# Where a two-network kernel splits three weight tiles, and 24 TensorE products that nobody reads

## The reference, cut to what matters

```
first network, layer l:
  mod = silu(c) @ w_ada[l] + b_ada[l]                  # shifts, scales, gates
  h = rms_norm(x) * (1 + scale_m) + shift_m
  x = x + gate_m * hybrid_mixer(h)                     # w_in, attention, gated linear attention, w_out
  h = rms_norm(x) * (1 + scale_f) + shift_f
  x = x + gate_f * moe(h)      # each token: one of 4 groups, 2 of its 8 experts
                               # an expert: (silu(h @ w_gate) * (h @ w_up) * weight) @ w_down
second network, layer l:
  x = x + mixer(rms_norm(x))                           # four kinds of attention, w_in_2, w_out_2
  x = x + relu(rms_norm(x) @ w_up_2)**2 @ w_down_2
```

## Time and profile before

| | |
|---|---|
| three timed runs | 1749.98, 1756.49, 1759.61 us; median 1756.49 |
| the profiled execution | 1746.62 us, of it a span of 1744.8 us |
| mean granted TensorE clock | 0.976 |
| busy over the span | PE 93%, DVE 67%, ACT 53%, POOL 6% |
| the two expert loops | some 300 us each (about 250 to 553 and 765 to 1066) |
| HBM traffic | 389 MB read, 224 GB/s over the span |

### The profile page before, as it was taken

The page is one execution under the profiler, slowest core; times in us unless marked ns, Lnnn a source line. Parts: engine busy times, 40 slices in busy tenths (PEclk is TensorE's granted clock), DMA queues, the critical chain, the costliest instruction groups (busy, mean ns, idle before and its releaser), DMA issues.

```text
span 1744.8 us, 24864 instructions
## 1 busy us (share of the span) xinstructions
PE 1630.8 (93%) x10344; PEld 1392.6 (80%) x10344; DVE 1173.4 (67%) x1380; ACT 929.5 (53%) x1192; POOL 96.9 (6%) x68
## 2 busy tenths in 40 slices
PE   6999989999997999889999998998999999989997
PEld 3677678888886677678888887887999987879996
DVE  2543678888887644778888887775655576855554
ACT  3361456666665452466666665445544443644442
POOL 0200000101010200000101101010000011000000
PEclk9999989999998999999999999999999999999999
DMA  8868618988986667249898886243465541535551
GB/s 320 300 221 299 230 69 338 331 334 326 341 316 238 231 233 259 97 145 343 326 343 318 336 330 210 70 167 128 149 196 186 181 122 34 185 98 192 193 193 60
DMA packets 132533, 392.11 MB, mean 225 GB/s; under 512 B 23360, under 2 KB 36672, under 8 KB 107840
## 3 DMA queue, kind: packets, MB, share of 16 engines
q1 hardware_dynamic: 131840, 388.35, 63.0%
q10 hardware_dynamic: 576, 2.10, 0.4%
HBM read 389.37 MB, written 1.05 MB: 224 GB/s over the span
## 4 chain that ended last, share of the span: by engine, by line
PE 75%; DVE 17%; ACT 3%; DMA 2%; issue 1%; POOL 1%; SPq 0%; POOLq 0%; ACTq 0%; DVEq 0%
PE ps L1156 18%; PE ps L468 12%; PE ps L2137 10%; DVE spl L369 10%; PE ps L448 5%; PE ps L1637 4%; PE ps L1661 3%; PE ps L511 2%; PE ps L634 2%; PE ps L527 2%; PE ps L1613 2%; PE ps L1682 2%; DVE ar L1344 1%; PE ps L1697 1%; PE ps L1181 1%
## 5 line engine op out<-in xcount | busy, mean ns | idle before, releaser
L369 DVE TENSOR_TENSOR spl<-ring,spl 128x2048 fp32r<-128x2048 f32 x255 | 586.8, 2320 | 138.5 <-ACT spl L360 138.5
L360 ACT ACTIVATE spl<-ring 128x2048 fp32r<-128x2048 f32 x254 | 486.8, 1916 | 205.0 <-PE ps L468 107.8
L1156 PE MATMUL ps<-spl,ur 128*128 128x256 f32 x3072 | 384.0, 282 | 25.2 <-DVE spl L369 23.9
L1156 PEld LDWEIGHTS ps<-spl,ur 128*128 128x128 f32 x3072 | 362.7, 189 | 43.7 <-DVE spl L369 36.8
L468 PEld LDWEIGHTS ps<-hh,spl 128*128 128x128 f32 x1728 | 205.3, 190 | 7.7 <-issue 5.9
L468 PE MATMUL ps<-hh,spl 128*128 128x256 f32 x1728 | 207.5, 281 | 2.8 <-DVE hh L431 2.8
L1181 PE MATMUL ps<-spl,hh 128*128 128x512 f32 x768 | 186.5, 392 | 2.0 <-DVE hh L1352 2.0
L2137 PE MATMUL ps<-spl,ur 128*128 128x512 f32 x768 | 176.7, 389 | 0.0
L808 DVE TENSOR_TENSOR spl<-ring,spl 128x1024 fp32r<-128x1024 f32 (+2 forms) x126 | 146.3, 1188 | 36.9 <-ACT spl L799 36.0
L2137 PEld LDWEIGHTS ps<-spl,ur 128*128 128x128 f32 x768 | 143.2, 188 | 29.2
L799 ACT ACTIVATE spl<-ring 128x1024 fp32r<-128x1024 f32 (+2 forms) x128 | 124.3, 1014 | 75.2 <-PE ps L448 23.8
(11 more groups left out here) (358 smaller groups left out, 1719.2 us busy)
## 6 DMA issues: line engine op xcount, KB each, us to landing
ring<-in_w_up SPq DMA_DIRECT2D x96, 1024.0 KB, 5.4
ring<-in_w_down SPq DMA_DIRECT2D x96, 1024.0 KB, 5.0
ring<-in_w_gate SPq DMA_DIRECT2D x64, 1024.0 KB, 5.6
ring<-in_w_ada SPq DMA_DIRECT2D x48, 1024.0 KB, 7.2
ring<-in_w_in SPq DMA_DIRECT2D x34, 1024.0 KB, 6.8
ring<-in_w_out SPq DMA_DIRECT2D x16, 1024.0 KB, 7.6
ring<-in_w_in SPq DMA_DIRECT2D x8, 384.0 KB, 3.6
gate<-in_b_ada ACTq DMA_DIRECT2D x4, 512.0 KB, 4.8
```

What stands on the lines that cost most here:

```text
L360: sc.activation(t.hi, t.raw, ACT.Copy).then_inc(s_hi, 2)
L369: v.tensor_tensor(t.lo, t.raw, t.hi, ALU.subtract).then_inc(s_lo, 1)
L1156: ins = pe.matmul(ps[:, 2 + e % 2, 256 * z:256 * z + 256], le, ri, start=(k == 0 and j == 0 and z == 0), stop=(k == 7 and j == 2), skip_gr ...
```

## The change

VectorE splits one tile more in the front of each expert stage, ahead of its wait for the experts' weights. Both engines' splits of the next stage's first tile leave the top of round 32: ScalarE's goes behind the loop, VectorE's into the next stage. `pe_spin` issues plain float32 products of the identity with a table of 512 columns into a PSUM bank that nobody reads then: 4 before the first network's second mixer waits for `xn`, and in each expert stage 4 before `xn`, 2 before the group choice, 1 before the places, 3 before the overflow branch. That is 24 products, of two instructions each.

```diff
+        def pe_spin(pe, bank, n):
+            for _ in range(n):
+                pe.matmul(ps[:, bank, :], ident, C("swa"), start=True, stop=True, skip_group_check=True)
@@ pe_mix1
+            if l:
+                pe_spin(pe, 0, 4)
             pe.wait_ge(*g(s_xn, 2))
@@ dve_mix1
             dve_norm(v, g, 2 * l, (3, 1) if l else (2, 2))
+            if l:
+                dve_lo(v, after_experts(0))
@@ pe_moe
+            pe_spin(pe, 7, 4)
             pe.wait_ge(*g(s_xn, 2))
...
             ins.then_inc(s_rt[2], 1)
+            pe_spin(pe, 0, 2)
             pe.wait_ge(*g(s_rt[3]))
...
+            pe_spin(pe, 0, 1)
             pe.wait_ge(*g(s_pl))
...
+            pe_spin(pe, 4, 3)
             pe_rest(pe, l)
@@ act_moe
             for e in range(33):
                 q = e % 2
-                if e == 32:
-                    act_hi(sc, after_experts(l))
...
+            act_hi(sc, after_experts(l))
             act_rest(sc, l)
@@ dve_moe
             dve_slots(v, l, 7)
+            dve_lo(v, last)
             v.wait_ge(s_cb, l + 1)
...
             for e in range(33):
                 q = e % 2
-                if e == 32:
-                    dve_lo(v, after_experts(l))
@@ dve_mix2
             v.tensor_reduce(m2.lam[:, 0:2], m2.tl.rearrange("p (a b) -> p a b", b=32), AX.X, ALU.add).then_inc(s_dl, 1)
+            if l == 0:
+                dve_lo(v, after_experts(1))
             dve_hT(v, g, PR(f"n1{l}"), last, 1)
```

## The result

| | before | after |
|---|---|---|
| timed beside each other, four runs each: median (lowest to highest) | 1755.83 us (1749.98 to 1759.61) | 1700.16 us (1698.21 to 1701.8) |
| ratio, 95% interval | | 0.9689 (0.9672 to 0.9706) |
| profiled execution (us), its span, its mean granted clock | 1746.62, 1744.8, 0.976 | 1698.64, 1696.8, 0.985 |

The kernel is 55.7 us faster by the medians.

A forecast was written before the change was run, and what follows sets the result against it. TensorE, busy 93% of the span, was taken as the bound, waiting mostly for VectorE's splits. 18.0 + 12.0 + 6.9 - 1.2 = 35.7 us off the 1756.5 median gave 1720.8 us, range 1706 to 1739.

The forecast's parts named there:

- change 1: Expert loops: VectorE's extra front split shortens each ordinary expert from 9.12 to 8.67 us; 18.0 us less over two stages.
- the gating's ring: Ordinary expert: a closed chain of products, SiLU, gating and VectorE's gate split, summing to the 9.12 us period.
- Group ends: Three experts at a group end take 28.7 us, with 0.8 kept for GpSimd; 2.0 less each, 12.0 for six.
- The front's split hidden: Stage fronts: the added split's 2.3 us lie beside TensorE's products of the expert weights, so they cost nothing.
- rival a: Expert loops: the weight transfers pace the experts at about 8.95 us a period; 1738 us in all; chance 0.14.
- (c): Expert loops: the new split order does nothing, something else holds 9.12 us; 1751 us in all; chance 0.05.
- (d): Expert loops: VectorE waits for unlanded tiles ahead of the gating; slower from a 9.5 us period, 1766; chance 0.04.
- The products: Fronts and second mixer: unread products in TensorE's waits keep its clock up; 5.4 and 1.5, together 6.9 us less.
- rival b: Stage ends: the jump over the overflow branch comes only behind the unread products; 5.2 us more, 1726; chance 0.07.
- The moved tile: First stage end 0.4 us sooner, other network's first mixer 2.28 us uncovered, partly returned by clock; net 1.2 us slower.
- The base: Whole kernel: 35.7 us subtracted from the timed median 1756.5, with the profiled execution 9.9 us below that median.

## Why the prediction was wrong, step by step

- **The failing step** is the one that sized change 1: "That makes 5.76 + 2.76 + 0.15 = 8.67, or 0.45 less", and with it "the upper is the 18.0 itself, since TensorE's own work fills 8.67". The 5.76 was not TensorE's own work. It held 0.22 of a stall at the up tile, and expert 1 of the same trace shows 5.54. Without the stall: 5.54 + 2.76 + 0.14 = 8.44, or 0.68 less. There are 21 such periods in a loop, not 20: 42 x 0.68 = 28.6 in place of 18.0. The bound was wrong with the term, so the range ended too high. The gain from the order was seen, and its cause half seen: the gating's ring was taken for the only one, when the ring through a1 was the longer one. Its sum came to 9.12 because the 5.93 held the other ring's stall. Opening the first gave nothing (1.0012), opening the second alone gave 19.1, and the front's split, which opens both, 45.6.
- **Group ends**: 6 x 2.25 = 13.5 against 12.0, with a wait of 1.03 for GpSimd where 0.8 was kept. Right. With the 28.6 it makes 42.1; in the first traces the starts of expert 1 and of the last down products are 42.7 closer together than before, over both stages.
- **The front's split hidden**: right, by the run of it alone. **The transfers keep up** (rival a): right, a DMA share of 0.90 and a median landing of 5.3. Rivals (c) and (d) fell with the periods of 8.44.
- **The products**: 6.9 forecast, 9.8 measured alone. In that run, transposes to expert 1 took 32.4 in each stage, in the two executions of before 34.1 to 35.5: some 2.6 a stage, 5.1 in all, where 5.4 was forecast. The gathers went from 6.19 to 4.29 (4.33 in the changed kernel), not to 3.8. The first network's second mixer, from its transposes to those of the next stage, gave 2.4 to 2.9, where 1.5 was forecast. What was not in the sum are the stage ends: priced at nothing, the first gave 0.5 to 3.1 (12.50 against 13.04 and 15.59 from the last down products to the transposes), the second 1.8 to 2.5.
- **The jump** (rival b): the forecast took nothing, a choice between two cases. It was right that the stages do not grow. A rule of the Trainium skill (Runtime: NRT & Kernel Launch, Instruction fetch mechanics), a fetch behind a taken branch whose target is not in the fetched window, agrees with an idle stretch there; by it, with the jump behind the products, the sum would have been 5.2 smaller, and that is not what came. At the second stage's end the products lie over part of that time: 4.3 to 6.6 of issue in the five kernels without them (5.00 and 5.33 in the two executions of before), 1.84 and 1.7 in two of those with them and a wait of 0.8 to 1.3 for VectorE in the others. The prediction leaned on the 3.1 at the first stage's end, all of it VectorE's; in the second execution of before that place shows 4.86 of issue too. That the jump is what makes this idle time was argued from its place; no run here moved or removed it.
- **The moved tile**: -1.2 forecast, +3.0 measured alone, at the limit of what can be measured. The +2.3 was right in place and size (the wait grew by 2.20). Missing was the clock behind that wait, 1.4 to 1.9 on the 96 products (12.62 to 13.09, where the first trace of before has 11.19). The 0.4 at the first stage end did not show in that run; in the changed kernel this stretch is 11.70, without the front's split 12.51. The 0.8 between them came with the split in the front, and why is not shown.
- **The base**: 48.0 lie between the two first profiled executions, 55.7 between the medians. The profiled one of before lay 9.2 below its median, that of after 1.5. The prediction subtracted from the median, and so this did not add to its error in the time; it hid some of the gain from the traces, above all because before's period itself varies (9.12 in most of one execution, 9.1 to 9.2 in the other) while after's is 8.44 in both, but for three experts of the second (up to 9.05).

What the sum should have been, by the parts: 28.6 + 13.5 + 9.8 - 3.0 = 48.9, from 1755.8 to 1706.9. 6.7 us of the gain are not settled. Part can be the measurement: by the ratios all three parts together gave 54.6 in one comparison and 52.6 in the other. The traces show where else it can lie. The loops of before, from expert 1 to the last down products, are 1.3 and 1.0 longer in its second execution. The first stage end is 13.04 in one execution of before and 15.59 in the other, and 11.70 and 11.71 in the changed kernel. The mixer behind it, from its transposes to those of the next stage, takes 171.6 to 172.3 in the six traces without the products and 168.0 to 171.2 in the six with them: the changed kernel has 171.07 in one execution, with the clock below 1.00 in windows at 600 and 644, and 168.01 in the other, without that.

## What to carry to other kernels

When an engine's wait disappears from a ring, the next bound is the same work in a place where nothing can wait inside it. Take that duration from a stretch in which all operands had been ready long before, as that of expert 1 here (5.54 against 5.76): a late operand in the middle of 48 pipelined products shows as 0.2 us of length and as no wait. And where two rings of almost one length close on the same engine, as 9.12 and 8.9 here, opening the shorter gives nothing. So list for each split what stands ahead of it and by how much it comes early, before putting all of the gain down to the one wait that shows.

## What the runs showed of the hardware

- A stall between pipelined products can leave no idle time in the records. In the trace of before each tenth of a microsecond from 276.5 to 277.1 has three of an expert's products in flight, and at 277.1 to 277.3, behind the end of the up tile's split at 276.98, two:

```profile
277.00:277.10 0.10, 0.10 (x3) 1.00 1.16 492
277.10:277.20 0.10, 0.10 (x2) 1.00 0.97 410
277.20:277.30 0.10, 0.10 (x2) 1.00 0.97 410
277.30:277.40 0.10, 0.10 (x3) 1.00 1.16 492
```

- The granted clock fell to 0.50 on TensorE work whose busy share is 4.00 of 4.00 us (the windows at 1083 and 1087 above), and in the changed kernel for some 3 us behind a wait of 2.82 that followed transposes at the full clock. What decides it, these runs don't show.
- The idle stretch behind the jump over the overflow branch is no fixed cost: at the second stage's end 4.32, 5.00, 5.33, 5.92, 6.40 and 6.61 in kernels without the products, and at the first stage's end none in one execution of before, 4.86 in the other and 4.90 with the up split moved.
